# Opening stage of a two-layer encoder kernel: scales of all rows first, shifts afterwards

## What is computed

```python
cond = silu(c)                                   # one vector of 1024
mod = cond @ ada_w[l] + ada_b[l]                 # 9 vectors of 1024: sh1, sc1, g1, sh2, ...
h = rmsnorm(x, g) * (1.0 + sc1) + sh1
gate, up = split(h @ w_in, 2)
x = x + 0.5 * g1 * (silu(gate) * up) @ w_out
```

## Time and profile before

| | |
|---|---|
| three runs | 2326.40, 2326.56, 2329.39 us, median 2326.56 |
| the profiled execution | 2326.26 us, span 2324.6 us |
| granted clock, mean | 0.997 |
| TensorE (PE) busy | 2298.4 us, 99% |
| VectorE (DVE) busy | 1282.3 us, 55% |
| ScalarE (ACT) busy | 850.3 us, 37% |
| GpSimd (POOL) busy | 113.3 us, 5% |

### The profile page before, as it was taken

One profiled execution on the slowest core, in us unless ns is written; L12 is line 12 of the kernel. 1 busy time (PEld: TensorE's weight loads), 2 busy tenths in 40 slices (PEclk: granted clock), 3 DMA queues, 4 the chain that ended last, 5 costly groups with the idle time before them and its releaser, 6 DMA issues.

```text
span 2324.6 us, 37188 instructions
## 1 busy us (share of the span) xinstructions
PE 2298.4 (99%) x14326; PEld 1866.9 (80%) x14326; DVE 1282.3 (55%) x1838; ACT 850.3 (37%) x1275; POOL 113.3 (5%) x220
## 2 busy tenths in 40 slices
PE   8999999999999999999999999999999999999998
PEld 6888888777777888888878888887777788888886
DVE  4554556686456664433465545667656577443334
ACT  5221234532455443223343222345225555321232
POOL 1000010020000000000000000001000000000000
PEclk9999999999999999999999999999999999999999
DMA  8564563343334345433345645623332352453331
GB/s 330 185 215 154 176 200 124 108 139 102 98 112 155 103 138 152 144 103 100 96 144 182 208 144 190 217 92 109 112 103 91 123 179 92 146 170 100 92 111 59
DMA packets 95156, 325.35 MB, mean 140 GB/s; under 512 B 12904, under 2 KB 13576, under 8 KB 94016
## 3 DMA queue, kind: packets, MB, share of 16 engines
q1 hardware_dynamic: 57456, 216.09, 28.5%
q0 software_dynamic: 23760, 82.48, 11.4%
q10 hardware_dynamic: 13824, 25.17, 3.1%
HBM read 306.34 MB, written 14.73 MB: 138 GB/s over the span
## 4 chain that ended last, share of the span: by engine, by line
PE 91%; DVE 5%; ACT 2%; DMA 1%; issue 1%; SPq 0%; DVEq 0%; POOL 0%; ACTq 0%; POOLq 0%
PE PS L547 80%; PE PS L1117 4%; PE PS L828 1%; DVE h L1778 1%; DMA ada<-in_ada_first_dram 1%; DVE wl L1567 1%; DVE t_buf L1805 0%; PE PS L1091 0%; ACT wh L1195 0%; PE PS L1134 0%; PE PS L747 0%; PE PS L1051 0%; PE PS L1100 0%; DMA ada_raw<-in_ada_w_dram 0%; PE PS L1067 0%
## 5 line engine op out<-in xcount | busy, mean ns | idle before, releaser
L1567 DVE TENSOR_TENSOR wl<-raw,wh 128x1024 fp32r<-128x1024 f32 (+2 forms) x360 | 466.2, 1295 | 776.0 <-ACT wh L1195 775.4
L547 PE MATMUL PS<-uh,wh 128*128 128x512 f32 x2176 | 860.8, 396 | 1.9 <-DVE wl L1567 1.4
L547 PE MATMUL PS<-ul,wh 128*128 128x512 f32 x2176 | 848.1, 390 | 0.0
L547 PE MATMUL PS<-uh,wl 128*128 128x512 f32 x2176 | 847.7, 390 | 0.0
L1195 ACT ACTIVATE wh<-raw 128x1024 fp32r<-128x1024 f32 (+2 forms) x360 | 401.8, 1116 | 868.4 <-PE PS L547 850.7
L547 PEld LDWEIGHTS PS<-uh,wh 128*128 128x128 f32 x2176 | 408.3, 188 | 97.9 <-issue 6.0
L547 PEld LDWEIGHTS PS<-uh,wl 128*128 128x128 f32 x2176 | 408.5, 188 | 86.5
L547 PEld LDWEIGHTS PS<-ul,wh 128*128 128x128 f32 x2176 | 408.7, 188 | 80.9
L547 PE MATMUL PS<-hh,wh 128*128 128x512 f32 x736 | 287.0, 390 | 0.0
L547 PE MATMUL PS<-hl,wh 128*128 128x512 f32 x736 | 286.4, 389 | 0.0
L547 PE MATMUL PS<-hh,wl 128*128 128x512 f32 x736 | 286.3, 389 | 0.0
(11 more groups left out here) (286 smaller groups left out, 1620.2 us busy)
## 6 DMA issues: line engine op xcount, KB each, us to landing
raw<-in_ffn_in_dram SPq DMA_DIRECT2D x176, 512.0 KB, 3.6
ada_raw<-in_ada_w_dram POOLq DMA_DIRECT2D x144, 512.0 KB, 3.9
raw<-in_mix_in_dram SPq DMA_DIRECT2D x88, 512.0 KB, 3.6
raw<-in_ffn_out_dram SPq DMA_DIRECT2D x32, 768.0 KB, 4.4
raw<-in_ffn_out_dram SPq DMA_DIRECT2D x32, 640.0 KB, 3.9
g_in<-gates_dram ACTq DMA_DIRECT2D x48, 256.0 KB, 3.1
ada<-in_ada_first_dram SPq DMA_DIRECT2D x8, 1024.0 KB, 16.4
raw<-in_mix_up_dram SPq DMA_DIRECT2D x16, 512.0 KB, 3.7
```

The costliest lines, as they stand in the source:

```text
L547: mm = e.matmul(PS[:, bank, :], w[:, j % 2, k * P:(k + 1) * P], v[:, k, :], start=(k == 0 and w is wh and v is xh), stop=(k == K - 1 and w ...
L1567: TTo(wl[:, j % 2, 0:K * P], raw[:, j, 0:K * P], wh[:, j % 2, 0:K * P], ALU.subtract)\
```

## The change

All scales come first: the eight lots are sorted anew on the host, so that lots 0 to 3 hold the scales of rows 0 to 7 (two rows each) and lots 4 to 7 the shifts. Units 0 and 1 multiply rows that are normed and scaled but not shifted (ScalarE L1534 without the shift, VectorE `first_lo`), and get the shift as a column, as in the other stages. The shifted rows are then made in place (`shifted` on VectorE, `shifted_row` on ScalarE, `shifted_lo` on VectorE) and unit 2 is the first to use them. TensorE's order is written out in `opening_units`. `raw` 2 is loaded ahead of lots 6 and 7, and `cond` behind `raw` 3; the activation of `cond` and the table load ahead of it come at the end of ScalarE's opening.

```diff
@@ sync
-                                if j < 2:
-                                    ada_lot(j)
-                                elif j == 2:
-                                    for lot in range(2, ADA_LOTS):
-                                        if lot == 4:
-                                            e.dma_start(cond[:, :], a["c"].broadcast_to([P, KD * P]))\
-                                                .then_inc(cond_in.sem, 16)
-                                        ada_lot(lot)
+                                for lot in ((0,), (1,), (2, 3, 4, 5), (6, 7))[j]:
+                                    ada_lot(lot)
                                 load(0, 0, j, a[name + "_in"][j], KD)
+                            e.dma_start(cond[:, :], a["c"].broadcast_to([P, KD * P])).then_inc(cond_in.sem, 16)
@@ tensor
+            def opening_units(banks):
+                def row_there(k):
+                    e.wait_ge(yh_done.sem, k + 1)
+                    e.wait_ge(yl_done.sem, k + 1)
+
+                def rows(j, pair):
+                    unit(0, j, j, KD, banks[j], uh, ul, None if j else row_there, range(2 * pair, 2 * pair + 2), j == 1)
...
+                first_sums(0)
+                e.wait_ge(rstd_done.sem, rstd_done.at(0, 1))
+                spread()
+                first_sums(1)
+                rows(0, 0)
+                rows(0, 1)
+                first_sums(2)
+                rows(1, 0)
+                first_sums(3)
+                rows(0, 2)
+                rows(1, 1)
+                first_sums(4)
+                rows(0, 3)
+                rows(1, 2)
+                first_sums(5)
+                rows(1, 3)
+                first_sums(6)
+                first_sums(7)
+                e.wait_ge(first_mods.sem, ADA_LOTS // 2)
+                shift_sums()
@@ ffn of tensor
                         if (l, s) == (0, 0):
-                            first_pair(l, l * UNITS + n0, (0, 2), s)
-                            in_unit(0, 2)
+                            opening_units((0, 2))
                         else:
                             first_units(l, l * UNITS + n0, (0, 2), s)
-                            e.wait_ge(silu_done.sem, silu_done.at(l, base_f))
-                            third_unit(l, l * UNITS + n0, s, 1)
+                        e.wait_ge(silu_done.sem, silu_done.at(l, base_f))
+                        third_unit(l, l * UNITS + n0, s, 1)
@@ scalar
+            def scaled_row(k):
+                e.wait_ge(first_scale.sem, k // 2 + 1)
+                e.wait_ge(xn_done.sem, k + 1)
+                e.activation(uh[:, k, :], xn[k][:, :], ACT.Identity, scale=scale_eff[:, k:k + 1], bias=eps[:, 2:3])\
+                    .then_inc(yh_done.sem, 1)
+
+            def shifted_row(k):
+                if k < KD - 1:
+                    e.wait_ge(row_used.sem, k + 1)
+                else:
+                    multiplied(0, 1)
+                e.wait_ge(t_done.sem, k + 1)
+                e.activation(uh[:, k, :], xn[k][:, :], ACT.Copy).then_inc(uh_done.sem, 1)
 
             split(0, 0, 0, 0, KD)
+            for k in range(4):
+                scaled_row(k)
             split(0, 0, 0, 1, KD)
+            for k in range(4, KD):
+                scaled_row(k)
+            split(0, 0, 0, 2, KD)
+            for k in range(KD):
+                shifted_row(k)
             e.sem_inc(mods_done.sem, 1)
+            split(0, 0, 0, 3, KD)
+            e.wait_ge(cond_in.sem, 16)
+            e.activation(cond[:, :], cond[:, :], ACT.Silu).then_inc(cond_done.sem, 1)
@@ vector
             def first_lo(k):
+                e.wait_ge(yh_done.sem, k + 1)
+                e.wait_ge(first_scale.sem, k // 2 + 1)
+                STT(out=ul[:, k, :], in0=xn[k][:, :], scalar=scale_eff[:, k:k + 1], in1=uh[:, k, :], op0=ALU.mult,
+                    op1=ALU.subtract).then_inc(yl_done.sem, 1)
+
+            def shifted(k):
+                e.wait_ge(first_mods.sem, k // 2 + 1)
+                e.wait_ge(yl_done.sem, k + 1)
+                TS(xn[k][:, :], xn[k][:, :], scale_eff[:, k:k + 1], mod[:, k:k + 1], ALU.mult, ALU.add).then_inc(t_done.sem, 1)
+
+            def shifted_lo(k):
                 e.wait_ge(uh_done.sem, k + 1)
+                TTo(ul[:, k, :], xn[k][:, :], uh[:, k, :], ALU.subtract).then_inc(ul_done.sem, 1)
 
             split(0, 0, 0, 0, KD)
             e.wait_ge(rstd_mm.sem, 1)
             normed(0)
+            normed(1)
+            first_sums(0)
+            normed(2)
+            first_lo(0)
+            normed(3)
+            first_lo(1)
             first_sums(1)
+            normed(4)
+            first_lo(2)
+            normed(5)
+            first_lo(3)
             split(0, 0, 0, 1, KD)
+            first_sums(2)
+            normed(6)
+            first_lo(4)
+            normed(7)
+            first_lo(5)
+            first_sums(3)
+            first_lo(6)
+            first_lo(7)
+            first_sums(4)
+            shifted(0)
+            shifted(1)
+            first_sums(5)
+            shifted(2)
+            shifted(3)
+            split(0, 0, 0, 2, KD)
+            for k in range(4):
+                shifted_lo(k)
+            first_sums(6)
+            shifted(4)
+            shifted(5)
+            first_sums(7)
+            shifted(6)
+            shifted(7)
+            for k in range(4, KD):
+                shifted_lo(k)
+            shift_columns(0, 0)
+            split(0, 0, 0, 3, KD)
```

More of the change, by code:

```diff
@@ L41 @@
 UNITS = 180
-LAG = 3
 WAKE = 32
@@ L436, in ffn @@
                                 load(l, m0, j, a[name + "_in"][l * 44 + j], KD)
-                        norms = 0 if half or start else norm_index(l, first // SUB) + 1
+                        norms = 0 if half else stage_index(l, first // SUB) + 1
                         with e.Fori(1 - half, F // 2) as i:
@@ L1255, in use_in @@
                             e.activation(dst, h32[:, j // 2, :], ACT.Copy).then_inc(hh_done.sem, 1)
-                    apart = half == 0 and (l, s) != (0, 0)
+                    apart, opens = half == 0, (l, s) == (0, 0)
                     steps(e, l, first, 2 * F, KD, F, split, use_in, False, (lambda: None) if apart else None)
@@ L1698, in use_in, with roots @@
                             ada_next(l, i + ADA_MAIN // 2, j // 2)
-                    apart = half == 0 and (l, s) != (0, 0)
+                    apart, opens = half == 0, (l, s) == (0, 0)
                     n = first
-                    steps(e, l, first, 2 * F, KD, F, split, use_in, False,
-                          (lambda: times_root(l, n, (0, 2), (silu_s[:, 0, :], h32[:, 0, :]))) if apart else None)
+                    def roots():
+                        if not opens:
+                            times_root(l, n, (0, 2), (silu_s[:, 0, :], h32[:, 0, :]))
+                    steps(e, l, first, 2 * F, KD, F, split, use_in, False, roots if apart else None)
                     first += 2 * F
@@ L2170, in first_sums @@
                 e.wait_ge(ada_step.sem, 2 * k + 2)
-                TTo(mod[:, k:k + 1], ada_sum[:, k:k + 1], ada_b[:, k:k + 1], ALU.add).then_inc(first_mods.sem, 1)
-                STT(out=scale_eff[:, k:k + 1], in0=ada_sum[:, KD + k:KD + k + 1], scalar=norm_g[:, 0, k:k + 1],
-                    in1=scale_0[:, k:k + 1], op0=ALU.mult, op1=ALU.add).then_inc(first_mods.sem, 1)
+                if not scales:
+                    TTo(mod[:, d:d + 2], ada_sum[:, d:d + 2], ada_b[:, d:d + 2], ALU.add).then_inc(first_mods.sem, 1)
+                    return
+                for part in range(2):
+                    v = d + part
+                    last = STT(out=scale_eff[:, v:v + 1], in0=ada_sum[:, KD + v:KD + v + 1], scalar=norm_g[:, 0, v:v + 1],
+                               in1=scale_0[:, v:v + 1], op0=ALU.mult, op1=ALU.add)
+                last.then_inc(first_scale.sem, 1)
             def normed(k):
```

120 lines of the change are left out of this document (41 added, 79 removed).

## The result

The kernel after takes 2331.10 us (median of 22 runs, 2328.70 to 2334.31), the kernel before, run beside it, 2328.34 us (2325.15 to 2330.65). The ratio is 1.0012, its 95% interval 1.0007 to 1.0018: 2.8 us slower, inside the 0.2% that were set as the bound for "no change". The profiled execution took 2330.02 us against 2326.26 before, 3.76 us more.

A forecast was written before the change was run, and what follows sets the result against it. The prediction took VectorE's queue to bound the new opening. The profiled 2326.26 us + 1.5 (later start of unit 2) + 1.5 (clock after the wait) gave 2329.3 us, range 2325.6 to 2332.0.

The forecast's parts named there:

- Step 1: First four rows: TensorE has them at 20.6 to 25.4 us; lot 2's sums put back by 4 us or more.
- Step 2: TensorE full from 25.4 us: sums 5 end at 38.0 to 40.5 us, sums 6 and 7 at 42.5 to 44.
- the late clock: Full clock returns some us later than before in the opening; sums 5 end at 39.8 us, against 38.0 when early.
- Step 3: VectorE's queue behind sums 5: last shifts at 45.0 to 47.2 us, TensorE idle 2.5 to 3.5 us.
- Step 4: The column, 1.1 us, new on the path: unit 2's start moves +0.1 to +2.3 us, taken as +1.5.
- Step 5: TensorE's clock after the wait ahead of the column: a fall costs 0 to 3.4 us, taken as 1.5.
- Step 6: The opening's 2.00 us stall: cause not removed, can cost 0 to 2 us; 0.5 in the spread of Step 2.
- The part set at nothing: Late loads or splits, seen as holes in units after unit 4: counted as no cost.
- A: Transfers bound the opening: unit 2 at 39.2 us, 6.9 us earlier, total 2319.4 us; chance 0.05.
- B: Opening with clock back early, no stall, no fall after the wait: 2326.3 to 2327 us; chance some 0.15, within the forecast's 0.69.
- C: Late clock, stall of 1 to 2 us, long clock fall ahead of the column: 5.7 us, 2332.0 us; chance 0.13.
- D: Wait ahead of the column only replaces the old row chain: shift between -4.6 and +0.4 us; chance 0.12.

The follow-up runs named there:

- 2: Changed kernel with eleven small matmuls put in TensorE's wait ahead of the column: 2330.58 us, ratio 1.001 to the kernel before.
- 4: Changed kernel with the order of transfers of the kernel before on SP's queue: 2331.44 us, ratio 1.0012 to the kernel before.
- 1: Changed kernel with VectorE's sums of lots 6 and 7 directly behind the weight split of unit 2: 2328.07 us, ratio 0.9999 to the kernel before.
- 12: Changed kernel, eleven small matmuls in TensorE's wait ahead of the column, VectorE's first two `ada_main` sums moved behind unit 3's split: 2328.39 us, ratio 0.9998.
- 6: Kernel before with 32 tiny matmuls (64 records) added in TensorE's idle time at 12.3 us: 2331.49 us, ratio 1.0012 to the kernel before.
- 5: Kernel 1 with two `shifted_lo` ahead of lot 5's sums and two of ScalarE's `shifted_row` ahead of its split: 2329.33 us, ratio 1.0003.
- 10: Kernel 9 with eleven small matmuls around the sums of lot 1: 2326.39 us, ratio 0.9988 to the kernel before.
- 8: Kernel 5 with eleven small matmuls around the sums of lot 1: 2327.31 us, ratio 0.9997 to the kernel before.
- 3: Changed kernel with lot 2's sums ahead of rows 2 and 3 of unit 0 on TensorE: 2329.61 us, ratio 1.0007 to the kernel before.
- 9: Kernel 5 with VectorE's first two `ada_main` sums moved directly behind the split of unit 3: 2325.53 us, ratio 0.9987 to the kernel before.
- 7: Kernel 5 with 32 tiny matmuls added at about 12.5 us: 2332.27 us, ratio 1.0017 to the kernel before.
- 11: Kernel 9 with 32 tiny matmuls (64 records) behind units 2 and 3: 2329.45 us, ratio 1.0006 to the kernel before.

## Why the prediction was right, and where its steps were off

The sign and most of the number came from the mechanism that was named: VectorE's queue ahead of the last shifts, an idle TensorE before the column, and a clock that falls with it. These are 2.89 us of the profile's 3.86. The other 0.97 came from a place that the prediction did not have, and that the sum came near all the same is in part luck.

**Step 1** held to the half microsecond: rows at 20.3, 21.6, 23.8 and 25.0 us (20.6, 22.0, 24.1, 25.4), lot 2's sums at 25.90.

**Step 2** took the clock to come back at the same time as before or later, and left room for a stall. It came back at 23.8 us, sooner than before, and there was no stall of 2 us: sums 5 ended at 38.1, the early bound of 38.0. One sum in the step is off: from 38.0 us the last two rows of unit 1 (1.36 us by its own pitch) end at 39.4, not 40.6, and sums 6 and 7 then end at 41.4 and not 42.5. They ended at 39.6 and 41.6. Profiles of kernels in which TensorE does the same up to there (2 and 4) have the late clock, to 27.7 and 30.3 us, so the range of the step was real.

**Step 3** held: last shifts at 46.2, in the bounds of 45.0 to 47.2, though TensorE needs only the last `mod`, at 45.2. The wait was 3.63 us, 0.13 above the top of its range; with the right end of sums 7 in step 2 the early case gives 3.6. Kernel 1 shows the cause.

**Step 4** took +1.5 us and had +0.99. Of this 0.83 is the column at half clock, which belongs to step 5; by its own terms it was +0.16, at its lower end, because of the early clock.

**Step 5** took 1.5 us of 0 to 3.4. It was 0.83 in the column and 1.90 in unit 2, 2.73, nearer to the upper end. The comparison with the wait of 2.00 us that did nothing was the wrong neighbour; kernels 2 and 12 put the fall down to the idle time, as matmuls of no use in it keep the clock at 1.00. That the trace of the changed kernel has the fall agrees with the rule of the Trainium skill quoted in the prediction (TensorE: Matmul & The Clock Gate, HAM oscillation).

**Step 6** had only the opening in view and forecast 0.5 in a spread. The opening's 2.00 us did not come, which the step had not foreseen, and 0.97 came at 685 us. "The same number of instructions is read" was the step that failed: the column adds 64 records, and kernel 6 shows that 64 records alone bring the stall there (1.31). That such a stall is a refill of instructions is not shown by an edit, but the packets of the instruction queue fit it (see the last section). If it is one, the Trainium skill's "mostly hidden" (Runtime: NRT & Kernel Launch, Instruction fetch mechanics) disagrees with that row as well, again with full DMA engines (share 1.00 from 686.08 to 687.05 us).

**The part set at nothing** was the chain from VectorE's first `ada_main` sums by POOL's loads to the weight splits at 65 to 70 us. It cost the changed kernel nothing and the prediction nothing. But between unit 4 and 73 us it took 0.7, 4.3 and 2.0 us from kernels 1, 2 and 5 in their profiles, and it is a large part of why mending the wait alone brought little.

**The rivals.** A, the transfers: against it stand kernel 4, which undoes their order and has the changed kernel's median, and the wait of 3.63 us, nine us after lot 7. B had the early clock and the missing stall right, and not the fall. C, the slow side, had the right mechanism, fall and price (2.73 of its 3.4), but not the late clock together with it; kernel 4's profile has the late clock, and took 2332.53 us. D had nothing saved or lost; what was lost is the clock behind the wait, which it left out.

The sum: 0.16 + 2.73 + 0.97 = 3.86 in the profile, against 1.5 + 1.5 forecast. Two terms too low by 1.2 and 0.97 and one too high by 1.3 nearly cancel, and that is luck. The medians are 2.8 us apart, close to the forecast of 3.0, but the forecast stood on a profiled execution 2.1 us below the median of the 22 runs (the prediction had three runs and saw only 0.3), so 2329.3 us is 1.8 below the 2331.10 that were measured.

## What to carry to other kernels

When a change takes work off the transfers, write down the queue of each engine from the last transfer to the first full unit: here four `shifted_lo` and two `shifted`, which TensorE needed only after the column, stood ahead of small sums that all of TensorE waited for, and moving the sums ahead of them was worth 2.7 us at unit 2. Then ask what the time gained will meet next; the gain of the opening was only kept (kernel 10 against 5 and 8) when the buffers of a side chain 15 us later were freed earlier as well. An idle stretch can cost its length and the half clock behind it, so compare a new one with the nearest that did cost something, not only with one that did not.

## What was not expected of the hardware

The stalls that no engine and no data transfer ends ("issue" in TensorE's timeline). In the opening they took 0.40 to 2.89 us, in kernels 1, 3 and 6 to 12 and in the kernel before; at 685 us, 640 us behind the change, 0.67 to 1.47. They move with the number of records ahead: 64 more than before (kernels 1, 3, 4, 5, 6, 9 and the changed kernel) and 86 more (2, 8, 10, 12) bring the one at 685, 128 more take it away (7, and 11, where one appears at 1825 us).

The 16 KB packets of the instruction queue q8 fit this. Every such stall in the opening ends 1.3 to 1.6 us after one of them, and every one at 685 us 4.5 to 5.0 us after one. The place of the packet differs between the kernels. From 680 to 682 us after, and from 688 to 690 before, where none lies between 676 and 688 and TensorE had passed the place at 683.18:

```profile
q8 instruction: 1, 0.02, 4.5%
```

```profile
q8 instruction: 1, 0.02, 3.5%
```

Other packets, all six between 12 and 50 us of the changed kernel among them, pass without a stall of this kind, so what else it takes stays open. The DMA engines were busy to a share of 0.5 to 1.0 in these stalls, so they need not be full.

The half-clock stretch has no fixed length in these profiles: 3.4, 6.8 and about 10 us after nearly the same work. At half speed the differences (3.4 and some 6.6 us) are worth up to 1.7 and 3.3 us, if TensorE is busy throughout. That would be scatter between executions by itself, and one profile in each kernel is not enough to price a part of the opening; the medians of the runs and the distances within one profile were needed together. What decides between the lengths was not tested.
